# A streaming encoder step: copies of turned probabilities on two engines in both prompt halves, new values fetched on ScalarE's queue, outputs scaled tile by tile

## The reference

```python
u = rmsnorm(x, norm_g) @ w_in                      # q, k, v, z of both groups, and the forget logits
# group 0: s = q k^T / 8 + c_t - c_s (c: cumulative log forget), causal softmax, times v
p = softmax(where(mask, s + bias, -inf)); oa = p @ v
# group 1: z = q k^T / 8, strictly causal
log_1m = where(mask, log_sigmoid(-z), 0)
a = exp(log_sigmoid(z) + suffix_sum(log_1m));      ob = a @ v
y = x + concat(rmsnorm(oa) * silu(za), rmsnorm(ob) * silu(zb)) @ w_out;  rmsnorm(y, final_norm_g)
```

## Time and profile before

| what | value |
|---|---|
| three timed runs | 1217.55, 1220.44, 1226.89 us; median 1220.44 |
| profiled execution | 1224.03 us, span of its records 1222.2 us |
| granted TensorE clock, mean of the span | 0.964 of full speed |
| busy share of the span | PE 89%, PEld 75%, DVE 59%, ACT 36%, POOL 18% |
| DMA | 222.50 MB, mean 182 GB/s |
| chain that ended last, by engine | PE 65%, DVE 12%, DMA 9%, issue 8%, ACT 3% |

### The profile page before, as it was taken

One profiled execution on the slowest core, in us unless ns is written; L12 is line 12 of the kernel. 1 busy time (PEld: TensorE's weight loads), 2 busy tenths in 40 slices (PEclk: granted clock), 3 DMA queues, 4 the chain that ended last, 5 costly groups with the idle time before them and its releaser, 6 DMA issues.

```text
span 1222.2 us, 28388 instructions
## 1 busy us (share of the span) xinstructions
PE 1086.2 (89%) x11873; PEld 915.8 (75%) x11873; DVE 721.5 (59%) x1016; ACT 438.9 (36%) x819; POOL 221.0 (18%) x152
## 2 busy tenths in 40 slices
PE   5899999899899999689969999989878888869997
PEld 5888998788788788678848787767656666657885
DVE  4423555155355457477556616676779999964653
ACT  4412222112212222022222226666665655633421
POOL 3100000000000000011111008000023464435550
PEclk9999999899999999899989999999999999978999
DMA  7391667698797987888988767424422422211332
GB/s 198 99 241 38 178 208 225 244 337 225 310 332 294 321 280 253 223 306 307 247 318 287 251 209 231 99 71 91 87 44 44 78 50 46 95 35 53 108 133 86
DMA packets 152032, 222.50 MB, mean 182 GB/s; under 512 B 92264, under 2 KB 128104, under 8 KB 135536
## 3 DMA queue, kind: packets, MB, share of 16 engines
q1 hardware_dynamic: 131184, 201.98, 53.6%
q10 hardware_dynamic: 20736, 18.88, 4.5%
HBM read 197.17 MB, written 23.66 MB: 181 GB/s over the span
## 4 chain that ended last, share of the span: by engine, by line
PE 65%; DVE 12%; DMA 9%; issue 8%; ACT 3%; POOL 1%; SPq 1%; ACTq 0%; DVEq 0%; POOLq 0%
PE bank L727 23%; PE bank L1537 7%; PE bank L800 6%; PE bank L1068 5%; PE bank L1024 5%; PE bank L1044 4%; DMA v_ring<-in_cache_fox_v 4%; PE bank L840 3%; PE bank L1005 3%; DVE k_buf L623 2%; DMA x_in<-in_x_prompt 2%; PE bank L827 2%; DVE om L1233 2%; DVE q_cur L616 2%; DMA k_buf<-in_cache_sb_k 2%
## 5 line engine op out<-in xcount | busy, mean ns | idle before, releaser
L727 PE MATMUL bank<-w_hi,hT_hi 128*128 128x256 f32 x1152 | 339.3, 294 | 2.7 <-ACT u_out L443 1.8
L727 PE MATMUL bank<-w_lo,hT_hi 128*128 128x256 f32 x1152 | 329.8, 286 | 0.0
L727 PE MATMUL bank<-w_hi,hT_lo 128*128 128x256 f32 x1152 | 329.2, 286 | 0.0
L727 PEld LDWEIGHTS bank<-w_hi,hT_hi 128*128 128x128 f32 x1152 | 225.0, 195 | 12.3 <-issue 8.1
L727 PEld LDWEIGHTS bank<-w_lo,hT_hi 128*128 128x128 f32 x1152 | 225.2, 196 | 0.0
L727 PEld LDWEIGHTS bank<-w_hi,hT_lo 128*128 128x128 f32 x1152 | 224.9, 195 | 0.0
L443 ACT ACTIVATE u_out<-bank 128x256 f32<-128x256 f32 x144 | 55.1, 383 | 428.7 <-PE bank L727 427.7
L623 DVE STREAM_TRANSPOSE k_buf<-k_buf 128x2048 f32<-128x2048 f32 x64 | 144.4, 2287 | 31.7 <-DMA k_buf<-in_cache_fox_k 19.6
L1291 POOL TENSOR_TENSOR pr<-pr,om 128x1023 f32<-128x1023 f32 (+3 forms) x64 | 93.4, 1466 | 227.7 <-DVE om L1233 224.5
L1068 PE MATMUL bank<-pT,v_nat 128*64 128x128 f32 x1152 | 99.7, 287 | 6.8 <-issue 4.5
L1233 DVE TENSOR_TENSOR_SCAN om<-om 128x1024 f32<-128x1024 f32 (+3 forms) x64 | 100.2, 1565 | 3.5 <-ACT om L1156 2.8
(11 more groups left out here) (169 smaller groups left out, 1672.6 us busy)
## 6 DMA issues: line engine op xcount, KB each, us to landing
k_buf<-in_cache_fox_k SPq DMA_DIRECT2D x32, 1024.0 KB, 10.3
v_ring<-in_cache_fox_v SPq DMA_DIRECT2D x32, 1024.0 KB, 9.3
k_buf<-in_cache_sb_k SPq DMA_DIRECT2D x32, 1024.0 KB, 8.5
v_ring<-in_cache_sb_v SPq DMA_DIRECT2D x32, 1024.0 KB, 7.8
w_raw<-in_w_in SPq DMA_DIRECT2D x15, 1024.0 KB, 14.3
out<-u_out ACTq DMA_DIRECT2D x72, 128.0 KB, 6.0
k_nat<-out SPq DMA_DIRECT2D x32, 256.0 KB, 4.0
q_nat<-q_scratch SPq DMA_DIRECT2D x32, 256.0 KB, 4.9
```

Of the source, the lines that this page charges most:

```text
L727: mm = pe.matmul(bank[:, U + i % 2, 0:NCOL], a[:, k, hcols(s)], b[c % 2][:, k, :], start=(k == 0 and n == 0), stop=(k == KD - 1 and n == 2))
```

## The change

1. In the stick-breaking half, ScalarE takes the even `lr` and VectorE the odd, as in the forgetting half; TensorE's waits follow.
2. `load_vn` moves from SyncE's list to ScalarE's, with its waits, and the first fetch of each group comes one step later (47 and 101). The scores of sequences 9 and 10 come one piece later (99, 105), and what is derived from them too; the last value product of sequence 8 moves from 102 to 103.
3. In `store_o` of the forgetting half, one multiplication of four tiles by the broadcast reciprocals becomes four multiplications, each by a scalar per partition.

```diff
@@ -263,11 +263,11 @@
...
-        SCORES_AT = [33, 43, 53, 59, 66, 73, 79, 86, 92, 98, 104, 110, 116, 122, 128, 134]
+        SCORES_AT = [33, 43, 53, 59, 66, 73, 79, 86, 92, 99, 105, 110, 116, 122, 128, 134]
         TURN_P_AT = [36, 50] + [s + (2 if n < DB - 2 else 4) for n, s in enumerate(SCORES_AT[2:])]
...
             (s + 2, s + 2, s + 3, s + 5) if n < DB - 2 else (s + 2, s + 2, s + 3, s + 4) for n, s in enumerate(TURN_P_AT[2:])]
-        VALUES_AT[DB] = (98, 98, 99, 102)
+        VALUES_AT[DB] = (98, 98, 99, 103)
@@ -285,6 +285,10 @@
...
                     load_first((i - 10) // 2 if i < 24 else CH)
+                if i == 47:
+                    load_vn(0)
+                if i == 101:
+                    load_vn(DB)
                 for n in range(NU_D):
@@ -293,10 +297,6 @@
...
                         turn_o(n)
-                if i == 46:
-                    load_vn(0)
-                if i == 100:
-                    load_vn(DB)
                 for v in range(CH):
@@ -380,22 +380,11 @@
...
-            def load_vn(n):
-                g, b = n // DB, n % DB
-                if b == 0:
-                    for c in (2 * BLOCKS.index(2 + 4 * g), 2 * BLOCKS.index(2 + 4 * g) + 1):
-                        sp.wait_ge(u_stored[T * c % UO], 16 * (T * c // UO + 1))
-                if n:
-                    sp.wait_ge(dpv_done, n)
-                sp.dma_start(v_new[:], (svs if g else fvs)[b * DS:b * DS + DS]).then_inc(vn_loaded, 16)
-
             def values(n, c):
...
                     load_v(q)
-                if c == CH - 1 and n + 1 < NU_D and (n + 1) % DB:
-                    load_vn(n + 1)
@@ -408,7 +397,7 @@
...
-            overlap_steps(nothing, load_w=load_w, forget=forget, load_first=load_first, load_vn=load_vn, values=values,
+            overlap_steps(nothing, load_w=load_w, forget=forget, load_first=load_first, values=values,
                           scores=scores, load_rest=load_rest)
@@ -513,7 +502,21 @@
...
-            overlap_steps(piece, split_w=split_w, forget=forget, turn_p=turn_p, scores=scores, soften=soften)
+            def load_vn(n):
+                g, b = n // DB, n % DB
+                if b == 0:
+                    for c in (2 * BLOCKS.index(2 + 4 * g), 2 * BLOCKS.index(2 + 4 * g) + 1):
+                        act.wait_ge(u_stored[T * c % UO], 16 * (T * c // UO + 1))
+                if n:
+                    act.wait_ge(dpv_done, n)
+                act.dma_start(v_new[:], (svs if g else fvs)[b * DS:b * DS + DS]).then_inc(vn_loaded, 16)
+
+            def values(n, c):
+                if c == CH - 1 and n + 1 < NU_D and (n + 1) % DB:
+                    load_vn(n + 1)
+
+            overlap_steps(piece, split_w=split_w, forget=forget, load_vn=load_vn, turn_p=turn_p, values=values,
+                          scores=scores, soften=soften)
             for m in range(4):
@@ -1034,11 +1037,7 @@
...
-                    if g:
-                        if lr == 0:
-                            pe.wait_ge(pt_moved_act, NTR // 2 * 8)
-                        pe.wait_ge(pt_moved_dve, NTR // 2 * 8 + NTR * (h - 8) + lr - 1)
-                    elif later(h, 1) or lr >= 2:
+                    if later(h, 1) or lr >= 2:
                         pe.wait_ge(pt_moved_dve if lr % 2 else pt_moved_act, NTR // 2 * h + lr // 2)
@@ -1057,10 +1056,7 @@
...
                     if j % 4 == 0:
-                        if g:
-                            pe.wait_ge(pt_moved_dve, NTR // 2 * 8 + NTR * (h - 8) + lr + 1)
-                        else:
-                            pe.wait_ge(pt_moved_dve if lr % 2 else pt_moved_act, NTR // 2 * h + lr // 2 + 1)
+                        pe.wait_ge(pt_moved_dve if lr % 2 else pt_moved_act, NTR // 2 * h + lr // 2 + 1)
                     part = slice((j % 2) * HD, (j % 2) * HD + HD)
@@ -1180,14 +1176,11 @@
...
                         move_o(h, 0)
-                    if not g:
-                        for n in range(TRB[u]):
-                            if (TRA[u] + n) % 2 == 0:
-                                act.activation(*move_pt(act, p, hh, u, n), ACT.Copy).then_inc(pt_moved_act, 1)
-                            if u == MOVE_LAST_AT and n == 0 and later(h, 1):
-                                move_o(h - 1, 1)
-                    elif u == MOVE_LAST_AT and later(h, 1):
-                        move_o(h - 1, 1)
+                    for n in range(TRB[u]):
+                        if (TRA[u] + n) % 2 == 0:
+                            act.activation(*move_pt(act, p, hh, u, n), ACT.Copy).then_inc(pt_moved_act, 1)
+                        if u == MOVE_LAST_AT and n == 0 and later(h, 1):
+                            move_o(h - 1, 1)
@@ -1247,15 +1240,16 @@
...
                 else:
-                    inv = rowinv[:, base:base + 4, hh].unsqueeze(2).to_broadcast([P, 4, HD])
                     dve.tensor_tensor(dst, even, o_odd[:], ALU.add).then_inc(o_added, 1)
                     dve.wait_ge(o_added, 2 * h + half + 1)
-                    dve.tensor_tensor(dst, dst, inv, ALU.mult).then_inc(on_done, 1)
+                    for t in range(4):
+                        mv = dve.tensor_scalar(dst[:, t], dst[:, t], rowinv[:, base + t, hh:hh + 1], None, ALU.mult)
+                    mv.then_inc(on_done, 1)
...
                     for n in range(TRB[u]):
-                        if g or (TRA[u] + n) % 2 == 1:
+                        if (TRA[u] + n) % 2 == 1:
                             dve.tensor_copy(*move_pt(dve, p, hh, u, n)).then_inc(pt_moved_dve, 1)
@@ -1505,8 +1499,8 @@
...
                     pe.wait_ge(s_moved, NU * NHEAD)
-                    pe.wait_ge(pt_moved_act, NTR // 2 * 8)
-                    pe.wait_ge(pt_moved_dve, NTR // 2 * 8 + NTR * 8)
+                    pe.wait_ge(pt_moved_act, NTR // 2 * NHEAD)
+                    pe.wait_ge(pt_moved_dve, NTR // 2 * NHEAD)
                 else:
```

## The result

The changed kernel took 1237.05 us (median of 4 runs, 1235.48 to 1241.41), the kernel before 1221.46 us in the same comparison (4 runs). The ratio is 1.0118, 95% interval 1.0085 to 1.0151: 14.4 us slower, 10.4 to 18.4. The profiled execution took 1241.41 us (span 1239.6), 17.4 us more span than before. The forecast was 1219 in a range of 1203 to 1231, and 1237 lies above it. So one profile tells where time goes, and medians of several executions tell how much the whole costs.

A forecast was written before the change was run, and what follows sets the result against it. TensorE was taken to set the pace nearly everywhere, so only its idle time could be won. From the profiled execution, 1224.0 - 3 - 2 + 4 = 1223; the timed median lay 3.6 lower, so 1219 us, range 1203 to 1231.

The forecast's parts named there:

- Part 1, minus 3: Cached part: v_new on ScalarE's queue and scores later; 6 + 3 us won, 6 given back, bounds minus 12 to plus 5.
- (a): Cached part: keys of 10 queue behind step 99's weight chunk; their scores start near 511, 6 us earlier, one more piece done.
- (c): Cached part: v_new lies behind two pieces' stores on ScalarE's queue; a few us of wait at step 103 is hidden.
- 6 + 3 us: Cached part: gain from scores of 10 starting 6 us earlier, plus about 3 us for one more piece done.
- (b): Cached part: second key half of 11 issued behind step 108's weight chunk; 6 to 9 us new wait before its scores.
- Rival D: Cached part: keys of 11 queue behind step 108's chunk, costing 9.73 us and up to 3 more; 1230 in all, chance 0.15.
- rival E: Cached part: v_new's fetch gets no faster on the other queue and is waited for at step 103; 1223, chance 0.15.
- Part 2, minus 2: Stick-breaking half: alternating copies win 0.55 us in each of five steady heads; minus 2 us, bounds plus 2 and minus 18.
- The walk of one head: Stick-breaking half: scans and GpSimd products form the chain; moved copies save 0.55 us a head, with a new 0.85 us wait.
- an allowance of 0.4 us: Stick-breaking half: gain allowed for the first two heads together, which start in the change from one half to the other.
- Part 3, plus 4: Forgetting half: four scalings take 0.25 us more than one, fifteen of sixteen waited for; plus 4 us, bounds 1 and 9.
- The rule that it quoted for the scans: VectorE with two SBUF inputs and GpSimd lock shared ports for a whole instruction, whoever starts first; 3.47 against 2.01 us.

The follow-up runs named there:

- run 1: Only the v_new fetch moved to ScalarE's queue plus the later steps, against the kernel before: 1234.79 us, ratio 1.0072.
- run 5: v_new on ScalarE's queue and later steps, with sequence 11's second key half fetched at step 107, ahead of the weight chunk, against the kernel before: 1225.45 us, ratio 0.9966.
- run 11: Fetch and copy changes, keys of 11 at step 107, GpSimd waiting for the first scaling, one scaling kept, against the kernel before: 1224.86 us, ratio 0.9987.
- run 12: Whole change with four scalings, keys of 11 at step 107 and GpSimd waiting for the first scaling, against the kernel before: 1229.61 us, ratio 1.0040.
- mended runs: run 5, run 11 and run 12, which fetch the keys of 11 at step 107, ahead of the weight chunk: 1225.45, 1224.86 and 1229.61 us.
- run 6: Only the later steps, v_new still on SyncE's queue, against the kernel before: 1236.06 us, ratio 1.0075.
- run 7: Only v_new's move to ScalarE's queue, at the old steps, against the kernel before: 1227.65 us, ratio 1.0002.
- run 2: Only the copies alternating between ScalarE and VectorE in the stick-breaking half, against the kernel before: 1229.90 us, ratio 1.0014.
- run 3: Only the four scalings in place of one, against the kernel before: 1237.64 us, ratio 1.0076.
- run 4: Four scalings only, with GpSimd's four products of the output weights cut into eight pieces each, against the kernel before: 1234.60 us, ratio 1.0064.
- run 8: Four scalings only, written as TENSOR_TENSOR with the inverse broadcast instead of TENSOR_SCALAR, against the kernel before: 1236.32 us, ratio 1.0069.
- run 9: Four scalings only, with GpSimd waiting for the first half head's scaling before the last weight quarter, against the kernel before: 1228.14 us, ratio 1.0004.
- run 10: The kernel before with only GpSimd's wait for the first scaling added, against the kernel before: 1224.70 us, ratio 0.9996.

## Why the prediction was wrong, point by point

**What bounds the kernel** was read rightly: TensorE's waits carried every effect that the runs show.

**Part 1, minus 3: measured +8.8 (5.2 to 12.6).** The step that failed is (a) with (c), "the scores of 10 start near 511 instead of 516.68, 6 us earlier and with one more piece done". Its 6 + 3 us were to come from a v_new that is hidden, and v_new was waited for 6.6 us in run 1 and 9.6 in the change; the scores of 10 started at 518 and 521. I had written down the sign of it, the store that took 15.4 us, and still hid v_new behind late keys that were not late (0.42 us). How much of the 9 us was won shows where the keys are on time: the second stretch is 304.0 to 307.2 us in runs 5, 11 and 12 and 307.8 to 310.7 in the eight kernels with the old steps, 306.1 and 309.6 in the mean. So it was 3 or 4 us at most, and the sum of the first two stretches (737.9 to 738.8 against 736.5 to 742.6) shows none of it.

Step (b) was right in mechanism and place, and undersized: 6 to 9 us forecast, a wait of 11.4 measured. The second stretch with the late keys (315.9, 316.2, 313.8) is 9.2 us above that of the mended runs in the mean. Part 1 had no term for the clock behind a new wait, which was 0.56 of full speed for 7 us in run 1 and 1.00 before. Rival D named the wait and priced it at 9.73 and up to 3 more; it missed how little of the 9 us ahead of it would be won. The reason is in part the one that rival E gave: the fetch got no faster on the other queue (runs 6 and 7). The five transfers "at some 3 us each" of step (a) were never tested, since the keys of 10 were not what TensorE waited for.

**Part 2, minus 2: measured +1.7 (-1.6 to 5.0), by the stages -0.6 alone and -2.1 in the whole.** The walk of one head was right: the 896-wide scan takes 3.80 us, there is a new wait of 0.85 for oT, and steady heads are at 22.69 where I said 22.5. The term that was mis-sized is the change from one half to the other: an allowance of 0.4 us won became 0.9 lost in run 2 (75.3 us for the first three heads, 74.4 before) and 1.6 lost in run 11 (76.0), while run 12 won 0.5 (73.9).

**Part 3, plus 4: measured +9.3 (4.9 to 13.6).** Per half head I said 0.25 us; the four take 0.74 for 0.42, so 0.32, and with the halves near 0.35 on the path. Fifteen of them are 5.1: right in mechanism, off by 1. By the stages part 3 alone costs 11.9 us (11.1 and 0.8), and what is missing is 6.5 us of hold at the first. The prediction looked for scalings beside GpSimd's products from 903 us only, "held as they are now", and not at 758, where the scaling of before ended 0.24 us inside a product of 4.66 us. That the first scaling could be held is the term it put at nothing. The rule that it quoted for the scans was the one to apply there. Around the change from one half to the other three scalings are held before (1.88, 1.42 and 1.87 us), and there the four took 2.14, 1.68 and 2.13 us in run 3: held as they were, as forecast, and 0.26 longer.

**The rest of the sum.** 8.8 + 1.7 + 9.3 are 19.8 us, each with 3 to 4 us of uncertainty, against 14.4 (10.4 to 18.4) measured for all. By the stages it is 8.9 up to the maxima, 11.6 and -1.3 behind them, and -1.8 at the end, 17.4.

**The parts before 426 us** took 3.7 us more in the changed kernel's profile. Runs 2, 3, 4, 8, 9 and 10 leave the overlap as it was and reach the step at 426.6 to 434.0, so such a difference needs no edit. Whether the later fetch of the first v_new adds to it stays open: the seven kernels with some of part 1 reach it at 429.7 to 435.8. One place where the two profiles differ is the clock after a wait: in the 7 us from 311, behind a wait of 4.17 and 5.09 us for values, it was 0.76 of full speed before and 0.52 after, nearly all at the lower level, 1.2 GHz. The two windows, before, then after:

```profile
311.00:318.00 7.00, 7.00 (x144) 4.22 (x146) 0.35 (x1) 0.00 (x0) 0.00 (x0) 0.76 0.91 359
```

```profile
311.00:318.00 7.00, 6.53 (x85) 3.49 (x93) 0.35 (x1) 0.00 (x0) 0.00 (x0) 0.52 0.92 362
```

## What to carry to other kernels

When an instruction list is moved by a step, look at what else is issued within the steps that it now meets: one step put two key transfers behind a 1 MB weight chunk, which cost 9 us, and one step back for the keys alone gave them back, but for a wait of 3 to 4 us. When a short VectorE instruction is made several, look in the trace for every long GpSimd instruction that begins within a few tenths of a microsecond of it, because missing such a meeting by 0.2 us is luck, and a wait that orders the two was cheap here (-0.5 us, from -3.7 to 2.6). Read repeated stretches between fixed points of several profiles before a sum: here the first of five stretches varies by 8 us with no edit in it, and the third and fourth show effects below 1 us.

## What the runs showed of the hardware

A cast of GpSimd with one SBUF input held VectorE as its product did: a TENSOR_SCALAR that began in it took 1.06 us for 0.25 (run 3), one in run 4 up to 1.91, and a TENSOR_TENSOR that began at 763.88 in a cast that ended at 764.68 took 1.08 for 0.42 (run 7). Not so at its very end: scalings that began 0.10 and 0.17 us before a cast was over took 0.42 and 0.46 us (before and run 2). A held instruction goes on behind the instruction that holds it, and if it needs more than one instruction's time in all, as the four do, the next of GpSimd may come in between: the cast and then the product, 5.8 us in run 3. A scaling that began 0.09 us ahead of a product was not held, and the product took 4.74 us for 4.5 to 4.6 (run 1). Four TENSOR_SCALAR of 64 elements, unhindered, took 0.74 us, each 0.25 with starts some 0.17 apart ((0.74 - 0.25) / 3). Eight products of 256 elements took GpSimd 5.54 us where one of 2048 took 4.5. Behind TensorE's waits for the keys of 11, of 3.2 to 11.9 us, the granted clock of the next 7 us was 0.56 to 0.76 in all six kernels with the new steps; in the eight others, which have no such wait, it was 1.00.
